# Value pages of a paged attention step gathered four at a time by row index, and the suffix sum and key-window loads that go with it

## What is computed

```
k_all, v_all = past pages of the sample (page_table), then the new row
z = q.k / sqrt(64) + bias                       # per head, per past token
log_rest  = log_sigmoid(-z)
log_stick = reverse cumulative sum of log_rest over tokens - log_rest
a = exp(log_sigmoid(z) + log_stick)
out = a @ v                                     # 8 heads of 64 columns
```

## Time and profile before

| | us |
|---|---|
| median of 3 runs | 1235.5 (1235.11 to 1236.73) |
| the profiled execution's own time | 1240.13 |
| its span in the trace | 1238.5 |
| PE busy | 928.0 (75%) |
| DVE busy | 634.3 (51%) |
| POOL busy | 442.1 (36%) |
| ACT busy | 352.1 (28%) |
| bytes moved by DMA | 481.20 MB, mean 389 GB/s |

### The profile page before, as it was taken

The page is one execution under the profiler, slowest core; times in us unless marked ns, Lnnn a source line. Parts: engine busy times, 40 slices in busy tenths (PEclk is TensorE's granted clock), DMA queues, the critical chain, the costliest instruction groups (busy, mean ns, idle before and its releaser), DMA issues.

```text
span 1238.5 us, 14521 instructions
## 1 busy us (share of the span) xinstructions
PE 928.0 (75%) x3666; PEld 419.6 (34%) x3666; DVE 634.3 (51%) x1606; ACT 352.1 (28%) x959; POOL 442.1 (36%) x497
## 2 busy tenths in 40 slices
PE   2798994667676897994678778777777778777784
PEld 1343331345221245881223223333233323332231
DVE  3200101333555252502677777777777777777755
ACT  1000011344211201222333333233334443344333
POOL 2102333012354000111355545455444455544541
PEclk9898996678888998997899999999989999999986
DMA  9999999956799999999999999999989999999996
GB/s 366 421 395 383 389 413 386 401 234 247 247 383 380 306 337 349 402 386 388 409 427 421 427 427 428 427 428 428 427 369 427 427 427 427 427 427 423 428 427 271
DMA packets 83707, 481.20 MB, mean 389 GB/s; under 512 B 11881, under 2 KB 12234, under 8 KB 42322
## 3 DMA queue, kind: packets, MB, share of 16 engines
q0 software_dynamic: 57216, 366.03, 72.0%
q1 hardware_dynamic: 26450, 114.66, 25.0%
HBM read 477.40 MB, written 70.32 MB: 442 GB/s over the span
## 4 chain that ended last, share of the span: by engine, by line
DMA 38%; PE 33%; issue 11%; DVE 6%; ACT 6%; POOL 2%; POOLq 2%; SPq 1%; DVEq 0%; ACTq 0%
DMA R<-in_uv,idst 31%; PE ps L895 9%; PE ps L548 7%; PE ps L846 5%; DMA R<-in_sb_k 3%; PE ps L801 2%; PE ps L574 2%; POOL R L452 2%; DMA pages<-in_pages 1%; POOLq L285 1%; ACT wgt L1141 1%; DMA R<-in_wts 1%; DMA R<-in_sb_v 1%; DMA R<-in_uv,idec 1%; PE ps L516 1%
## 5 line engine op out<-in xcount | busy, mean ns | idle before, releaser
L895 PE MATMUL ps<-R,diag 128*128 128x512 f32 x1024 | 490.3, 628 | 162.8 <-ACT diag L1160 162.8
L452 POOL DMA_INDIRECT R<-in_uv,idst x256 | 313.3, 1224 | 358.6 <-PE ps L895 285.2
L1617 DVE CUSTOM_DVE_ANT_0 R<-R,H 128x1024 f32<-128x1024 f32 x264 | 319.3, 1223 | 193.9 <-DMA R<-in_uv,idst 182.7
L895 PEld LDWEIGHTS ps<-R,diag 128*128 128x128 f32 x1024 | 195.3, 199 | 457.8 <-ACT diag L1160 249.8
L1138 ACT ACTIVATE gel<-dots 128x2 f32<-128x2 f32 x132 | 26.8, 203 | 396.6 <-DVE dots L1617 396.6
L392 POOL DMA_DIRECT2D R<-in_wts x36 | 19.1, 530 | 243.9 <-PE ps L486 89.5
L548 PE MATMUL ps<-R,HT 128*128 128x512 f32 x192 | 93.3, 625 | 8.5 <-DMA R<-in_wts 8.5
L1160 ACT ACTIVATE diag<-const,wgt 128x128 f32<-128x128 f32 x256 | 88.8, 393 | 14.1 <-ACT wgt L1141 1.5
L676 PE MATMUL ps<-R,ast 128*32 128x512 f32 x256 | 56.1, 749 | 18.9 <-DMA R<-in_sb_v 17.9
L1141 ACT ACTIVATE wgt<-gel,gst 128x1 f32<-128x1 f32 x264 | 63.3, 287 | 4.3
L846 PE MATMUL ps<-HT,R 128*128 128x264 f32 x256 | 61.2, 400 | 0.7 <-ACT HT L926 0.7
(11 more groups left out here) (271 smaller groups left out, 839.7 us busy)
## 6 DMA issues: line engine op xcount, KB each, us to landing
R<-in_wts POOLq DMA_DIRECT2D x48, 1024.0 KB, 14.1
out_dil_k_s<-in_dil_k SPq DMA_DIRECT2D x32, 1023.5 KB, 8.4
out_dil_v_s<-in_dil_v SPq DMA_DIRECT2D x32, 1023.5 KB, 8.6
R<-in_sb_k SPq DMA_DIRECT2D x64, 256.0 KB, 7.9
R<-in_sb_k POOLq DMA_DIRECT2D x64, 256.0 KB, 6.2
R<-in_sb_v POOLq DMA_DIRECT2D x64, 256.0 KB, 5.5
R<-in_sb_v SPq DMA_DIRECT2D x64, 256.0 KB, 6.6
R<-in_uv,idst POOLq DMA_INDIRECT x256, 11.9
```

The costliest lines, as they stand in the source:

```text
L452: pool.indirect_dma_start(out=R[:, row_slot(k), :], out_offset=None, in_=A["uv"], in_offset=bass.IndirectOffsetOnAxis(ap=idst[:, par, k:k ...
L895: last = pe.matmul(ps[:, banks + q, :], diag[:, k % 4, :], R[:, row_slot(k), D + q * 512:D + (q + 1) * 512], start=False, stop=False, skip ...
L1617: dve.tensor_tensor_reduce(u, u, H[:, t, :], 1.0, 0.0, ALU.mult, ALU.add, dots[:, k:k + 1]).then_inc(s["dot_done"], 1)
```

## The change

The values of a sample now come in four gathers of 1 MB (`value_quad`). Each is an indirect DMA on POOL in which partition p takes one row of 8 KB, that is four adjacent tokens of one page: partition p of gather m holds tokens 4p to 4p+3 of the 512 tokens of pages 4m to 4m+3. The row numbers lie in `vrow`, a table of 128 by 32 integers: the host sends the page numbers, and DVE multiplies them by 32 and adds `place` (p % 32). All scores, weights and sums of the samples take the same order of tokens ("block 4m+u" is now every fourth token, at offset u). PE therefore turns the scores with a stride of four columns, and a partition's four blocks of a quarter are adjacent tokens. The suffix sum works on four quarters of 512 tokens: three additions of 256 columns inside the quarters, one of 768 columns into `z1`, three of 64 columns over the quarters, and two matmuls of 256 columns. `pages_pv` uses a gather with four matmuls and raises `v_used` once, and a gather waits for that.

The key windows are loaded by SP, in front of the value windows and behind the copies of pair 1, and POOL's list between the weights and the experts holds only gathers.

```
+VQ = NPG // 4
+        VS = (4, 5, 8, 9)
+        def zq(a):
+            return a.rearrange("p (m u n) -> p m u n", m=VQ, u=4)
...
-        def value_pages(eng, b, chunks, first=False):
-            for c in chunks:
-                page_chunk(eng, b, c, A["sb_v"], kv_ready,
-                           [(s["k_used"], (NB - 1) * CPB + c + 1)] if first else [(s["v_used"], b * CPB + (c - CPB + 1))])
+        def value_quad(b, m):
+            nc.gpsimd.indirect_dma_start(
+                out=R[:, VS[m], :], out_offset=None, in_=A["sb_v"],
+                in_offset=bass.IndirectOffsetOnAxis(ap=vrow[:, b * VQ + m:b * VQ + m + 1], axis=0),
+            ).then_inc(v_ready[m], 16)
...   (SP)
             sp.dma_start(pages[:, :], A["pages"]).then_inc(s["pages_in"], 16)
+            sp.dma_start(vrow[:, :], A["vrow"]).then_inc(s["pages_in"], 16)
             sp.dma_start(const[:, P:], A["consts"][:, P:]).then_inc(s["c_in"], 16)
-            sp.wait_ge(s["pages_in"], 16)
+            sp.wait_ge(s["pages_in"], 32)
...
-            value_pages(sp, 0, EVEN, first=True)
             copy_windows(1, 0)
-            with sp.Fori(1, NB) as b:
-                value_pages(sp, b, EVEN)
             sp.wait_ge(s["new_out"], 64)
+            sp.wait_ge(s["h_ready"], 3)
+            for b in range(NB):
+                if b >= 2:
+                    sp.wait_ge(s["dk_used"], b - 1)
+                window_rows(sp, DK, b, b % 2, A["dil_k"], A["dil_k_s"], dk_ready)
             sp.wait_ge(s["dk_used"], NB)
...   (POOL)
-            value_pages(pool, 0, ODD, first=True)
-            weight_rounds(6, 9)
-            pool.wait_ge(s["new_out"], 64)
-            pool.wait_ge(s["h_ready"], 3)
-            for b in range(2):
-                window_rows(pool, DK, b, b, A["dil_k"], A["dil_k_s"], dk_ready)
-            weight_rounds(9, 10)
...
-            with pool.Fori(1, NB // 2) as i:
-                windows_and_values(i)
-            value_pages(pool, NB - 1, ODD)
+            pool.wait_ge(s["rows_ready"], 1)
+            for m in range(VQ):
+                pool.wait_ge(s["k_used"], (NB - 1) * CPB + 2 * m + 2)
+                value_quad(0, m)
+            weight_rounds(6, 10)
+            for b in range(1, NB):
+                for m in range(VQ):
+                    pool.wait_ge(s["v_used"], (b - 1) * VQ + m + 1)
+                    value_quad(b, m)
             weight_rounds(10, CHUNKS // WSLOTS)
...   (PE)
-                last = pe.transpose(ps[:, 6 + n // 4, n % 4 * P:(n % 4 + 1) * P], zl[:, n * P:(n + 1) * P], ident)
+                last = pe.transpose(ps[:, 6 + n // 4, n % 4 * P:(n % 4 + 1) * P], zl[:, bass.ds(n // 4 * 512 + n % 4, P, step=4)], ident)
...
-                    for half in range(2):
-                        c = slice(half * 512, (half + 1) * 512)
-                        pe.matmul(ps[:, 3 + half, :], tri, zl[:, c], start=True, stop=False)
-                        last = pe.matmul(ps[:, 3 + half, :], ones, zt[:, c], start=False, stop=True)
-                    last.then_inc(s["z_s"], 1)
+                    pe.matmul(ps[:, 3, 0:VQ * PAIRS], tri, zq(zl)[:, :, 3, :], start=True, stop=False)
+                    pe.matmul(ps[:, 3, 0:VQ * PAIRS], ones, zt[:, 0:VQ * PAIRS], start=False, stop=True).then_inc(s["z_s"], 1)
...
+                for m in range(half * 2, half * 2 + 2):
+                    pe.wait_ge(v_ready[m], i * 16 + 16)
+                    for u in range(4):
+                        last = pe.matmul(quad(j, u), ast[:, j, 4 * m + u, :], R[:, VS[m], u * DG:(u + 1) * DG],
+                                         start=(m == 0), stop=(m == VQ - 1))
                     last.then_inc(s["v_used"], 1)
...   (DVE, behind the wait for qkv_ev 10)
+            dve.wait_ge(s["pages_in"], 32)
+            vrow_f = gall[:, 0:2, :].rearrange("p a n -> p (a n)")
+            step(dve.tensor_copy(vrow_f, vrow[:, :]))
+            step(dve.tensor_scalar(vrow_f, vrow_f, float(QUAD), cst("place"), ALU.mult, ALU.add))
+            dve.tensor_copy(vrow[:, :], vrow_f).then_inc(s["rows_ready"], 1)
...
-                    step(dve.memset(zt[:, 960:1024], 0.0))
-                    for n in range(NPG - 2, -1, -1):
-                        nxt = slice((n + 1) * 64, (n + 2) * 64)
-                        ins = dve.tensor_tensor(zt[:, n * 64:(n + 1) * 64], zl[:, nxt], zt[:, nxt], ALU.add)
+                    for u in range(1, 4):
+                        step(dve.tensor_tensor(zq(zl)[:, :, u, :], zq(zl)[:, :, u, :], zq(zl)[:, :, u - 1, :], ALU.add))
+                    step(dve.memset(zt[:, (VQ - 1) * PAIRS:VQ * PAIRS], 0.0))
+                    dve.tensor_tensor(zq(z1)[:, :, 1:4, :], zq(z1)[:, :, 1:4, :], zq(zl)[:, :, 0:3, :], ALU.add)
+                    for m in range(VQ - 2, -1, -1):
+                        nxt = slice((m + 1) * PAIRS, (m + 2) * PAIRS)
+                        ins = dve.tensor_tensor(zt[:, m * PAIRS:(m + 1) * PAIRS], zq(zl)[:, m + 1, 3, :], zt[:, nxt], ALU.add)
```

More of the change, by code:

```diff
@@ L115, in constants @@
     put("iota", np.tile(np.arange(TOPK, dtype=np.float32), (P, 1)))
+    put("place", (np.arange(P) % QUAD)[:, None].astype(np.float32))
     return c
@@ L169, in build @@
         pages = sb("pages", [1, NB * NPG], I32)
+        vrow = sb("vrow", [P, NB * VQ], I32)
         stat = sb("stat", [P, 32])
@@ L250, in build @@
         kv_ready = [sem(f"kv_ready{n}") for n in range(KVS)]
+        v_ready = [sem(f"v_ready{n}") for n in range(VQ)]
         dk_ready = [sem(f"dk_ready{n}") for n in range(2)]
@@ L416, in _ @@
                                    s4[(2 + q) * QUAD:(2 + q) * QUAD + NB, r, :]).then_inc(s["new_out"], 16)
-            value_pages(pool, 0, ODD, first=True)
-            weight_rounds(6, 9)
-            pool.wait_ge(s["new_out"], 64)
-            pool.wait_ge(s["h_ready"], 3)
-            for b in range(2):
-                window_rows(pool, DK, b, b, A["dil_k"], A["dil_k_s"], dk_ready)
-            weight_rounds(9, 10)
-            def windows_and_values(i):
-                for j in range(2):
-                    pool.wait_ge(s["dk_used"], i * 2 + (j - 1))
-                    window_rows(pool, DK, i * 2 + j, j, A["dil_k"], A["dil_k_s"], dk_ready)
-                    value_pages(pool, i * 2 - 1 + j, ODD)
-            with pool.Fori(1, NB // 2) as i:
-                windows_and_values(i)
-            value_pages(pool, NB - 1, ODD)
+            pool.wait_ge(s["rows_ready"], 1)
[7 more added lines that the diff above has]
+                    value_quad(b, m)
             weight_rounds(10, CHUNKS // WSLOTS)
@@ L671, in pages_pv @@
                     pe.wait_ge(s["ast_ready"], i + 1)
-                for c in range(half * 4, half * 4 + 4):
-                    pe.wait_ge(kv_ready[c % KVS], i * 32 + (NB + 1) * 32)
-                    for g in range(KVP):
-                        n = c * KVP + g
-                        last = pe.matmul(quad(j, n % QUADS), ast[:, j, n, :], KV[c % KVS][:, g, :],
-                                         start=(n < QUADS), stop=(n >= NPG - QUADS))
+                for m in range(half * 2, half * 2 + 2):
[3 more added lines that the diff above has]
+                                         start=(m == 0), stop=(m == VQ - 1))
                     last.then_inc(s["v_used"], 1)
@@ L1405, in page_rows @@
             def page_rows(i, j, first=False):
-                block_rows(i, j, first, s["v_used"], CPB, s["msk_ready"], s["oA_mm"], P)
+                block_rows(i, j, first, s["v_used"], VQ, s["msk_ready"], s["oA_mm"], P)
             def dilated_pair(g, first=False):
@@ L1728 @@
         "sb_k": head_pairs(a["cache_sb_k"]),
-        "sb_v": a["cache_sb_v"].reshape(-1, P, DG),
+        "vrow": np.repeat(a["page_table"].reshape(NB * VQ, 4).T, QUAD, 0),
+        "sb_v": a["cache_sb_v"].reshape(-1, 2 * D),
         "dil_k": a["cache_dil_k"].reshape(NB, PAST * DG),
```

14 lines of the change are left out of this document (7 added, 7 removed).

## The result

| | before | the change |
|---|---|---|
| median | 1236.12 us (4 runs, 1235.11 to 1242.77) | 1254.73 us (4 runs, 1254.08 to 1255.66) |
| ratio to before | | 1.014, 95% interval 1.0103 to 1.0176 |
| span of the profiled execution | 1238.5 us | 1252.3 us |
| PE busy | 928.0 us | 929.6 us |
| DVE busy | 634.3 us | 634.4 us |

What follows compares the result with a forecast made beforehand. The prediction took DMA as the bound after 316 us, its start set by the PE, ACT and DVE chain. Terms summed to -4.4 us, taking the median from 1235.5 to 1231.1 us; the range ran from just past 1221 to 1241.

Steps and rivals of the forecast that it cites:

- the equation at its head: Time of the end: moment the busy stretch begins, plus DMA work left, plus any idle time of the queues.
- the three rivals: POOL the real pace: 1222.4 us, chance 0.14; lead eaten: about 1235, 0.20; four slots too few: 1247, 0.18.
- Start: SP and POOL also wait for `vrow`, so key pages and a weight slip: +0.5 us, ends 0 and +1.5.
- Turned scores: Eight PE transposes read `zl` with a stride of four columns: +0.3 us, ends 0 and +2.
- Suffix and clock: Suffix sum shorter on DVE (-0.9 us) and PE (-4.6); PE's next transposes and scores at a lower clock (+0.6).
- Restart: Sample 1's stream restarts only after a whole gather is used, not one chunk: +0.5 us, ends 0 and +1.
- Values and depth: Samples 1 to 7: values in 8 KB rows move faster, -1.8 us; four 1 MB slots replacing eight chunks, +1.0.
- the rival that had POOL as the pace: Value stage: POOL's issue chain was the bound; -10.5 us in place of -1.8, median 1222.4 us, chance 0.14.
- Four slots too few: Value stage: PE's absences leave queues empty some 2.4 us per sample; +17 us instead of +1, median 1247, chance 0.18.
- the rule against it: POOL's value gathers can starve for descriptors while DVE holds shared ports; the sum put held issues inside 0.95 to 1.99 us.
- Key windows on SP: Key windows leave POOL's list, and value windows of samples 0 and 1 come earlier; same work, 0 us.
- an expert stage that begins no earlier though the chain is shorter: Sign of a wrong forecast: the end would not hang on the moment when the queues fill.

Runs made afterwards that it cites:

- the longer suffix: The aligned change with three more 512-column matmuls on PE and four more DVE additions between turned scores and first gather: 1233.97 us, ratio 1.000.
- the aligned change: The change plus 480 unused bytes per partition behind the constants, so R begins at a multiple of 512 again: 1229.22 us, ratio 0.9959; repeated, 1229.18 us, 0.9955.
- the two aligned runs: The aligned change timed twice without further edit: first 1229.22 us, ratio 0.9959; second, on another chip, 1229.18 us, ratio 0.9955.
- the 32 bytes: The kernel before with 32 unused bytes per partition behind the constants: 1256.78 us, ratio 1.0177.
- the version that doesn't wait: The aligned change with `vrow` on its own semaphore behind the constants, so SP and POOL wait only for the page numbers: 1231.06 us, ratio 0.998.
- the three aligned kernels: The aligned change twice (1229.22 and 1229.18 us) and once with value windows issued late (1226.36 us).
- with 256 and with 512 bytes: The kernel before with 256 or 512 spare bytes per partition behind the constants: 1234.51 us, ratio 1.0008, and 1236.06 us, ratio 1.0022.
- halved gathers: The aligned change with two gathers of 4 KB rows for each of 8 KB, half slots released separately: 1241.92 us, ratio 1.0063.
- the windows late: The aligned change with SP issuing the value windows only after the last but one sample's pages are used: 1226.36 us, ratio 0.9942.

## Why the prediction was wrong

**The step that failed** is the second term of the equation at its head: the end is "the moment at which the busy stretch begins, plus the DMA work left". The equation itself stands, as the longer suffix showed. But I took the DMA work left as bytes over 427 GB/s and gave the change terms for order, rows and depth only. The time of one and the same transfer had no term, though the diff shows a new column in the first tensor of a list that is laid out in order. None of the three rivals held this either. The missing term is +1.84% by the ratios (1.014 against 0.9957), 22.6 us, and the sum without it was -4.4. With the address restored the change measures 1229.2 us; 0.9957 of 1235.5 is 5.3 us less than before. The time that the forecast gave to this change belongs to the aligned one, and that -5.3 comes so near to -4.4 is partly luck: the terms below were off in both directions.

Its size can be read from the packet records. In the change and in the aligned change the median record of 8 KB takes 313 and 309 ns, one of 4 KB (POOL's key pages) 169 and 159, one of 2 KB on SP's queue 87 and 84. The pieces of the window copies, which don't land in SBUF, show no such step (2460 ns in the change, 2426 and 2440 in the two aligned runs, 2461 and 2452 in the kernel before without and with the 32 bytes). Summed up and divided by 16 engines the three sizes take 14.9, 1.8 and 5.2 us more in the change than in the first aligned run, 21.9 us in all beside the 22.6. Why a record costs 3 to 10 ns more is not shown.

**Start**, +0.5: `vrow` lands at 27.00 us, later than the 24 to 24.5 that I gave it, and yet nothing is lost, since the version that doesn't wait isn't faster: DVE begins to scale the scores at 202.60, 206.29 and 203.43 us in the three aligned kernels with the wait, and at 207.27, 203.30 and 203.37 in the old code with the address in place (as it was, with 256 and with 512 bytes). The term should have been 0.

**Turned scores**, +0.3: the eight strided transposes take 1.23 us together at a granted clock of 1.00. The 1.97 of the earlier trace rows stood at 0.50; the old code at 1.00 (with 512 bytes) takes 1.09, and the strided ones at the lower level (halved gathers) take 1.98. So the stride costs 0.14 us at most.

**Suffix and clock**, -0.9 -4.6 +0.6 = -4.9: from the end of the DVE step that forms `zl` to the end of the second pair's first score matmuls. The chain of the kernel before shows it, with its `L616` and `L617` in that place, and the last of these rows is the end of the stretch:

```profile
235.20 1.15 DVE Z L1327
...
247.88 0.71 PE ps L616 x4
248.59 0.25 PE ps L617 x4
```

That is 236.35 to 248.84, 12.5 us. In the change the same stretch runs from 238.39 to 246.95:

```profile
245.26 1.23 PE ps L620 x4
246.49 0.46 PE ps L621 x4
```

8.6 us, so -3.9; in the aligned change it runs from 231.24 to 239.08, 7.8 us, -4.6. The size was right. The clock came as priced: in both the transposes behind the short matmuls take 1.06 us at a granted clock of 0.50, where the kernel before has 0.60 at 1.00. The score matmuls behind them took 1.69 us in the change, still at 0.50, and 0.97 in the aligned one, back at 1.00, as against 0.96 behind the long ones.

**Restart**, +0.5: in the aligned change the first gather of sample 1 is issued 1.4 us behind the first value matmul; the first page was issued 2.8 us behind it, the matmul being at 313.89. Not a cost. Its timeline on POOL:

```profile
305.16 0.99 POOL L305 DMA_INDIRECT R<-in_sb_v,vrow  x1 [17.00 <-PE ps L677]
306.45 0.97 POOL L305 DMA_INDIRECT R<-in_sb_v,vrow  x1 [0.30 <-issue]
```

Together these bring the first value matmul from 310.3 us, the mean of three executions with the old code and full rate (313.89, 308.65, 308.40), to 305.1. That is -5.2, where start, scores, suffix and clock came to -4.1. Single executions differ by 5 us here, so a comparison of only one pair (313.89 and 312.01) would have misled. Counted from the end of the step that forms `zl`, the scatter is smaller: the first value matmul comes 76.2 to 77.6 us behind it in the old code, 72.6, 71.2 and 72.6 in the three aligned kernels, 73.6 in the change and 76.8 with the longer suffix.

**Values and depth**, -1.8 +1.0: the stage from the first value matmul to the last use takes 98.1 us before, 102.4 and 101.0 in the aligned change, and 93.2 with the windows late. The last has the same bytes in the stage as the kernel before (34.6 and 34.5 MB), moved at 372 GB/s instead of 352 at a DMA share of 0.98 and 0.99, so like for like it is -4.9, between my forecast of -0.8 and the -10.5 of the rival that had POOL as the pace. It doesn't show that POOL was the pace. The rows are enough: before, half of the pages came as records of 2 KB (84 ns at the median, so 336 ns for 8 KB) and half as records of 4 KB (159, so 318), now 8 KB take 309. For 29.4 MB that is 4.0 us (an estimate from these medians), and I had 1.8 because I took the rate of the pages from a window of 2 us.

"Four slots too few" did not come true: the share of the stage is 0.98 in the change and was 0.99 before, and no 17 us are lost. Two of the signs that I gave for it did appear, waits just over 3 us at the weight loads and a median gather that lands after 12.1 us, but the kernel before had waits of up to 3.3 us too, and the experts' gathers land after 11.9 us in full queues, so these signs don't tell an empty queue from a full one. As for the rule against it: 4 of the 32 gathers of the change took more than 1.1 us, the longest 1.90 (937 ns at the least, 939 at the median), together 2.3 us above the median. By that rule ("SBUF — State Buffer", section "SBUF: two separate sides", of the Trainium skill) DMAs of this queue can starve while DVE holds the shared ports. Whether DVE held these four up no run shows, and a loss of that size in the value stage isn't seen.

**Key windows on SP**, 0: the windows of samples 0 and 1 of the values do move in front of the last pages, as the text said, and the last page is used 7.7 us later by it, while the end moves by at most 2.

**What would show it** named a sign that came near: "an expert stage that begins no earlier though the chain is shorter". The experts' first gather is issued at 529.31 us, before at 519.94, and the first that the chain waits for lands at 592.21, before at 593.39. But the prediction took the sign to mean that the end doesn't hang on the moment when the queues fill, and the longer suffix shows that it does. The sign that would have told, the rate of the experts' stage at a full share, was not on the list.

## What to carry to other kernels

When a change adds or widens a tensor, look at where the tensors behind it land: in a kernel bound by its DMA, destinations that began 32, 64 or 128 bytes behind a multiple of 256 bytes of a partition cost 1.4 to 1.8% here, more than the change itself was worth. If the rate at a full busy share differs between two profiles, ask for the cost of the single transfer before asking about order and waits. And put new small tensors at the end of the list, or pad, so that a comparison measures the change and nothing else.

## What the runs showed of the hardware

- A shift by 32, 64 or 128 bytes of the destination in SBUF takes the gathers of 8 KB rows from 427 GB/s down to between 420 and 422, and a record of 8 KB from 309 to 312 or 313 ns, at the same DMA share of 1.01; 256 and 512 bytes cost nothing. The Trainium skill ("DMA: Bandwidth & Descriptors", section "How a descriptor splits into AXI transactions") says that a transaction must start at a 256-byte boundary, and that an unaligned start costs beats for the bytes below it. The boundary of 256 agrees with these runs. By that account, as an estimate, the waste in beats would grow with the offset, one beat of 32 bytes on top of the 256 of an 8 KB row for 32 bytes and four for 128, so 0.4% and 1.6%; measured are 1.6% and 1.2%, so it doesn't grow. The number of transactions would be flat, 33 instead of 32 at each of these offsets, but no run shows what a transaction costs. That passage speaks of reads, where here the writes are off.
- A software DMA on POOL took 0.94 us, and 0.30 us to the next, whether its 128 rows had 4 or 8 KB, so halving the gathers doubled POOL's time and put it on the chain.
- At the same bytes larger rows load the DMA engines less: the records of 2, 4 and 8 KB took 84, 159 and 309 ns at the median, which is 336, 318 and 309 ns for 8 KB.
